# Gated scan in a two-block transformer kernel: the level products below 32 kept as strips of 32 keys, the two highest levels written without selection

## The reference

```python
def chunk_gated_scan(q, k, v, log_f, s0, with_output):
    ...
        decay = jnp.exp(jnp.where(causal, bcum[:, :, None] - bcum[:, None], -jnp.inf))
        scores = jnp.einsum('bthk,btshk,bshk->bhts', qc, decay, kc)
        o = jnp.einsum('bhts,bshv->bthv', scores, vc) + jnp.einsum(
            'bthk,bhkv->bthv', qc * jnp.exp(bcum), state)
...
    o_lf, _ = chunk_gated_scan(ql, klf, il, llf, s_cf, True)
    o_lb, _ = chunk_gated_scan(flip(ql), flip(klb), flip(il), flip(llb), s_cb, True)
```

## Time and profile before

| what | value |
|---|---|
| median of 3 runs | 2749.49 us (2744.36 to 2750.85) |
| the profiled execution, its own time | 2755.42 us |
| its span, first to last instruction | 2753.3 us |
| PE busy over the span | 2437.4 us (89%), 13690 records |
| DVE, ACT, POOL busy | 1002.5, 734.5, 198.6 us |
| mean granted PE clock | 0.910 |
| the changed block | 424.5 to 531.1 us |

### The profile page before, as it was taken

One profiled execution on the slowest core, in us unless ns is written; L12 is line 12 of the kernel. 1 busy time (PEld: TensorE's weight loads), 2 busy tenths in 40 slices (PEclk: granted clock), 3 DMA queues, 4 the chain that ended last, 5 costly groups with the idle time before them and its releaser, 6 DMA issues. The chain is left out here.

```text
span 2753.3 us, 32259 instructions
## 1 busy us (share of the span) xinstructions
PE 2437.4 (89%) x13690; PEld 1839.1 (67%) x13690; DVE 1002.5 (36%) x1585; ACT 734.5 (27%) x1271; POOL 198.6 (7%) x239
## 2 busy tenths in 40 slices
PE   6979999987999988996687999998986777799997
PEld 3533456775888866886665888886864555588885
DVE  2013118533333334635124333423225543343333
ACT  2122200023222222313212322322213552332331
POOL 0000006400000000012000000000022440000000
PEclk8988999888999997997558999998997998899999
DMA  6120013311223111200011222212210003122210
GB/s 281 38 90 17 21 41 131 145 46 47 105 79 122 69 70 62 92 31 2 4 62 62 92 92 92 92 64 92 92 33 1 1 1 123 61 92 94 110 72 31
DMA packets 16110, 196.33 MB, mean 71 GB/s; under 512 B 1888, under 2 KB 3040, under 8 KB 3936
## 3 DMA queue, kind: packets, MB, share of 16 engines
q1 hardware_dynamic: 15392, 190.72, 18.5%
q10 hardware_dynamic: 576, 3.56, 0.3%
HBM read 190.08 MB, written 2.10 MB: 70 GB/s over the span
## 5 line engine op out<-in xcount | busy, mean ns | idle before, releaser
L1503 DVE TENSOR_TENSOR wsp_mlp<-ring,wsp_mlp 128x1024 fp32r<-128x1024 f32 x128 | 156.7, 1225 | 447.8 <-ACT wsp_mlp L1474 447.8
L1474 ACT CAST wsp_mlp<-ring 128x1024 fp32r<-128x1024 f32 x128 | 133.9, 1048 | 491.4 <-PE psum L1459 489.4
L1456 PE MATMUL psum<-hs_mlp,wsp_mlp 128*128 128x512 f32 x512 | 201.7, 394 | 36.2 <-DVE wsp_mlp L1503 36.2
L1456 PE MATMUL psum<-acts_mlp,wsp_mlp 128*128 128x512 f32 x512 | 202.4, 395 | 0.0
L1458 PE MATMUL psum<-hs_mlp,wsp_mlp 128*128 128x512 f32 x512 | 201.3, 393 | 0.0
L1459 PE MATMUL psum<-hs_mlp,wsp_mlp 128*128 128x512 f32 x512 | 201.1, 393 | 0.0
L1459 PE MATMUL psum<-acts_mlp,wsp_mlp 128*128 128x512 f32 x512 | 199.3, 389 | 0.0
L1458 PE MATMUL psum<-acts_mlp,wsp_mlp 128*128 128x512 f32 x512 | 199.2, 389 | 0.0
L1503 DVE TENSOR_TENSOR wsp_ffn<-ring,wsp_ffn 128x1024 fp32r<-128x1024 f32 x66 | 80.8, 1225 | 246.2 <-ACT wsp_ffn L1474 246.2
L414 PE MATMUL psum<-hsev,wspev 128*128 128x512 f32 x672 | 156.6, 395 | 0.4 <-DVE arena_low L1647 0.3
L1456 PE MATMUL psum<-hs_ffn,wsp_ffn 128*128 128x512 f32 x352 | 138.1, 392 | 19.5 <-DVE wsp_ffn L1503 19.5
(11 more groups left out here) (391 smaller groups left out, 4152.9 us busy)
## 6 DMA issues: line engine op xcount, KB each, us to landing
ring<-weights SPq DMA_DIRECT2D x85, 2048.0 KB, 7.9
ring<-weights SPq DMA_DIRECT2D x3, 1024.0 KB, 5.7
cst<-consts ACTq DMA_DIRECT2D x1, 2209.0 KB, 14.3
xT<-xin SPq DMA_DIRECT2D x2, 1024.0 KB, 7.2
out<-xT SPq DMA_DIRECT2D x1, 2048.0 KB, 6.3
ring<-weights SPq DMA_DIRECT2D x1, 1280.0 KB, 5.9
mixT<-ctxin ACTq DMA_DIRECT2D x1, 1024.0 KB, 15.5
ring<-weights SPq DMA_DIRECT2D x2, 512.0 KB, 3.4
```

What stands on the lines that cost most here:

```text
L1456: pe.matmul(tile_bank(g, j), w_hi, src[:, 0, k0 + i, :], start=(first and i == 0), stop=False)
L1474: act.copy(wsp[:, q % 2, 0, :], raw_view(q)).then_inc(s["w_hi"], 1)
L1503: dve.tensor_tensor(wsp[:, q % 2, 1, :], raw_view(q), wsp[:, q % 2, 0, :].bitcast(F32), ALU.subtract).then_inc(s["w_lo"], 1)
```

## The change

Levels 0 to 4 keep their scores compact. A pair of halves at these levels lies within 32 tokens, so of a 128x128 chunk only the four diagonal 32x32 blocks are needed. The new tensor `w_near` (128 x 4 heads x 128) holds them: partition 32r+a is key a of strip r, column 32i+b is query b of chunk i. `near` makes them with 32 matmuls a unit, each 32 keys against 16 queries of one strip in one direction. The predicated copy goes over 128 columns with a 128x32 table `pair{lev}`. The diagonal product is made in the same layout by 16 matmuls a head instead of 4.

Levels 5 and 6 (`far`) need no selection: 16 matmuls of 32x32 and 8 of 64x64 a unit write exactly the wanted blocks into the head's bank `h`, where they stay. Ahead of level 5, `nearest` brings the compact blocks of the head to their places in the same bank, with 16 matmuls by slices of the identity. At the end ACT copies the four full banks to `wsc`. DVE no longer has a predicated copy at levels 5 and 6.

The products that update the keys are put in a helper `keys`, called by POOL with the same operands and in the same order. The arena grows by 512 columns, and the tables have 5 x 32 columns where they had 7 x 128.

```diff
+    for lev in range(5):
+        m = level_mask(lev, True) + level_mask(lev, False)
+        out[f"pair{lev}"] = np.concatenate([m[32 * r:32 * r + 32, 32 * r:32 * r + 32] for r in range(4)], axis=0)
...
+        def keys(eng, lev, h):
+            k1, _ = halves(kk[:, 0, h, :], lev)
+            _, _, (_, t2) = products_of(ff[:, 0, h, :], lev)
+            eng.tensor_tensor(k1, k1, t2, ALU.mult)
+            _, k2 = halves(kk[:, 1, h, :], lev)
+            _, _, (t1, _) = products_of(ff[:, 1, h, :], lev)
+            eng.tensor_tensor(k2, k2, t1, ALU.mult).then_inc(k_upd, 1)
...
-                        dve.wait_ge(sel_done, u - 3)
...
-                    mask = C(f"cross{lev}").bitcast(U32).rearrange("p (o n) -> p o n", o=1).to_broadcast([P, TT, P])
-                    dve.copy_predicated(wsc[:, h, :].rearrange("p (i n) -> p i n", i=TT), mask,
-                                        bank(u % 4).rearrange("p (i n) -> p i n", i=TT)).then_inc(sel_done, 1)
+                    if lev < NEAR:
+                        if lev >= 1:
+                            dve.wait_ge(sel_done, u - 3)
+                        mask = C(f"pair{lev}").bitcast(U32).rearrange("p (o n) -> p o n", o=1).to_broadcast([P, TT, 32])
+                        dve.copy_predicated(w_near[:, h, :].rearrange("p (i n) -> p i n", i=TT), mask,
+                                            bank(u % 4, P).rearrange("p (i n) -> p i n", i=TT)).then_inc(sel_done, 1)
...
-                    act.wait_ge(qf_set, h + 1)
-                    act.wait_ge(qb_set, h + 1)
-                    act.copy(wsc[:, h, :], bank(4 + h % 2)).then_inc(w_set, 1)
+                    act.copy(w_near[:, h, :], bank(4 + h % 2, P)).then_inc(w_set, 1)
                 for ch in range(4, 12):
                     mod_copy(act, ch)
+                for h in range(HH):
+                    act.wait_ge(lev_done, NU - HH + h + 1)
+                    act.copy(wsc[:, h, :], bank(h))
...
+                def near(lev, h, out):
+                    for i in range(TT):
+                        for d in (0, 1):
+                            for r in range(4):
+                                rows = slice(32 * r, 32 * r + 32)
+                                sl = slice(i * P + 32 * r, i * P + 32 * r + 32)
+                                to = halves(out[rows, 32 * i:32 * i + 32], lev)[1 - d]
+                                last = pe.matmul(to, kk[:, d, h, sl], halves(q_dec[d][:, h, sl], lev)[1 - d],
+                                                 start=True, stop=True)
+                    return last
+
+                def far(lev, h, out):
+                    half = 1 << lev
+                    for i in range(TT):
+                        for r in range(P // half):
+                            d = r % 2
+                            to = half * (r + 1 - 2 * d)
+                            last = pe.matmul(out[half * r:half * r + half, i * P + to:i * P + to + half],
+                                             kk[:, d, h, i * P + half * r:i * P + half * r + half],
+                                             q_dec[d][:, h, i * P + to:i * P + to + half], start=True, stop=True)
+                    return last
+
+                def nearest(h, out):
+                    for i in range(TT):
+                        for r in range(4):
+                            pe.matmul(out[32 * r:32 * r + 32, i * P + 32 * r:i * P + 32 * r + 32],
+                                      ident[:, 32 * r:32 * r + 32], w_near[:, h, 32 * i:32 * i + 32],
+                                      start=True, stop=True)
...
-                        pe.wait_ge(sel_done, u - 3)
-                    for i in range(TT):
-                        sl = slice(i * P, (i + 1) * P)
-                        out1, out2 = halves(bank(u % 4)[:, sl], lev)
-                        pe.matmul(out2, kk[:, 0, h, sl], halves(q_dec[0][:, h, sl], lev)[1], start=True, stop=True)
-                        last = pe.matmul(out1, kk[:, 1, h, sl], halves(q_dec[1][:, h, sl], lev)[0], start=True,
-                                         stop=True)
+                        pe.wait_ge(sel_done, min(u - 3, near_units))
+                    if lev == NEAR:
+                        nearest(h, bank(h))
+                    last = (near if lev < NEAR else far)(lev, h, bank(u % 4))
```

More of the change, by code:

```diff
@@ L100, in constants @@
     out["sooner_neg"] = np.where(a[:, None] <= a[None, :], 0.0, NEG).astype(np.float32)
-    for lev in range(LEVELS):
-        out[f"cross{lev}"] = level_mask(lev, True) + level_mask(lev, False)
+    for lev in range(5):
+        m = level_mask(lev, True) + level_mask(lev, False)
+        out[f"pair{lev}"] = np.concatenate([m[32 * r:32 * r + 32, 32 * r:32 * r + 32] for r in range(4)], axis=0)
     f32 = np.float32
@@ L238, in program @@
         epsc = sb("epsc", [P, 1])
-        ARENA = 22760
+        ARENA = 22760 + 512
         held = []
@@ L966, in program @@
         o_hg = sb("o_hg", [P, 2, T], s6)
+        w_near = sb("w_near", [P, HH, P], s6)
         k_sum = state.rearrange("p a b c -> p (a b c)")[:, 0:HH * T].rearrange("p (h n) -> p h n", h=HH)
@@ L1050, in program @@
             sem(n) for n in ("diag_done", "w_set", "qf_set", "qb_set", "lev_done", "sel_done", "q_upd", "k_upd", "t_upd"))
+        NEAR = 5
+        near_units = NEAR * HH
+        def keys(eng, lev, h):
[5 more added lines that the diff above has]
+            eng.tensor_tensor(k2, k2, t1, ALU.mult).then_inc(k_upd, 1)
         with nc.Block() as block:
@@ L1061, in _ @@
                         pool.wait_ge(k_upd, u - 3)
[L1062 to L1068, removed]
+                    keys(pool, lev, h)
             @block.vector
@@ L1093, in _ @@
                         dve.wait_ge(q_upd, u - 3)
-                        dve.wait_ge(sel_done, u - 3)
[L1095 to L1101, removed]
-                    mask = C(f"cross{lev}").bitcast(U32).rearrange("p (o n) -> p o n", o=1).to_broadcast([P, TT, P])
-                    dve.copy_predicated(wsc[:, h, :].rearrange("p (i n) -> p i n", i=TT), mask,
-                                        bank(u % 4).rearrange("p (i n) -> p i n", i=TT)).then_inc(sel_done, 1)
+                    _, q2 = halves(q_dec[0][:, h, :], lev)
+                    _, _, (t1, _) = products_of(ff[:, 0, h, 0:T], lev)
+                    dve.tensor_tensor(q2, q2, t1, ALU.mult)
+                    q1, _ = halves(q_dec[1][:, h, :], lev)
+                    _, _, (_, t2) = products_of(ff[:, 1, h, 0:T], lev)
+                    dve.tensor_tensor(q1, q1, t2, ALU.mult).then_inc(q_upd, 1)
+                    if lev < NEAR:
[4 more added lines that the diff above has]
+                                            bank(u % 4, P).rearrange("p (i n) -> p i n", i=TT)).then_inc(sel_done, 1)
                     if u >= 1:
@@ L1126, in _ @@
                     for i in range(TT):
-                        last = pe.matmul(bank(4 + h % 2)[:, i * P:(i + 1) * P], k_sum[:, h, i * P:(i + 1) * P],
-                                         hq[:, h, i * P:(i + 1) * P], start=True, stop=True)
+                        for r in range(4):
+                            sl = slice(i * P + 32 * r, i * P + 32 * r + 32)
+                            last = pe.matmul(bank(4 + h % 2)[32 * r:32 * r + 32, 32 * i:32 * i + 32], k_sum[:, h, sl],
+                                             hq[:, h, sl], start=True, stop=True)
                     last.then_inc(diag_done, 1)
```

## The result

The changed kernel takes 2732.3 us in the median (2726.4 to 2735.7, 6 runs) against 2745.8 for the kernel before on the same chip (2744.0 to 2750.9, 6 runs): ratio 0.9942, 95% interval 0.9928 to 0.9957. It is faster: 13.5 us by the medians, 12 to 20 us by the interval; 12.1 were forecast. The profiled execution is 2732.3 us (span 2730.3).

What follows compares the result with a forecast made beforehand. PE was taken as the bound, with DVE and POOL taking turns just under it. Savings of 3.4 + 9.7 + 0.4 - 2 + 0.6 = 12.1 us took the median from 2749.5 to 2737.5 us, range 2728 to 2750.

Steps and rivals of the forecast that it cites:

- The likeliest case: In the level loop the bound goes from PE to DVE and POOL taking turns: 12.1 us gained, chance 0.62.
- the signs that the prediction named for being wrong: POOL and DVE still waiting over 20 us for PE, pauses cutting the records, or granted clock under 0.9 in the stage.
- Levels 0 and 1: 8 x 0.43 = 3.4: In eight units where DVE was full, each select shortened by 0.43 us shortens the stage: 3.4 us off.
- the third rival: DVE gains little because its products meet POOL's and wait, 3 x 1.1 us: gain 6, 2743 us, chance 0.08.
- Levels 2 to 6: 9.7, less 2 for pauses: Twenty units at DVE's and POOL's turns take 58.6 us against 68.3; PE's pauses at chunk changes give 2 back.
- PE's price: Levels 0 to 4: 64 product records a unit at 0.015 us, 0.96 us against 1.79; 0.45 if record count cost nothing.
- the rival of instruction supply (0.13): PE stays the bound by its instruction count, 0.029 us a record with pauses every 128: gain 6.8, 2743 us, chance 0.13.
- The clock (0.17): Granted clock halves inside the stage: for part of it 2743 to 2750 us (0.10), for most of it slower (0.07).
- ACT's four last copies: Four 512-element copies at the stage's end, 0.58 us each, hidden beside DVE's and POOL's last units; uncovered, worth 0.8 us.
- The tables: 368 KB less to load in the opening stage: 0.6 us off, at most 0.88, at least nothing.
- The last turn: At the end of the level loop the last turn is no longer waited for: 0.4 us off.
- POOL's share: POOL's busy share of the level loop rises from 67% to over 75%.

Runs made afterwards that it cites:

- e2: The changed kernel with both products that update the keys moved from POOL to DVE: 2724.0 us, ratio 0.9930.
- e4: The kernel before with its predicated copy cut from 512 to 128 columns, leaving out three of four chunks' scores: 2744.5 us, ratio 1.0001.
- e5: The changed kernel with strips of 64 keys instead of 32 at levels 0 to 4, select over 256 columns: 2738.4 us, ratio 0.9967.
- e6: The changed kernel with strips of 64 keys at levels 0 to 4 and both key products on DVE: 2718.4 us, ratio 0.9886.
- e8: The changed kernel with the tables padded by 736 unused columns to their old size: 2727.3 us, ratio 0.9930.
- e3: The changed kernel with the products of levels 0 to 4 issued twice into the same place: 2759.0 us, ratio 1.0055.
- e1: The kernel before with only the products of levels 5 and 6 changed, levels 0 to 4 as before: 2737.1 us, ratio 0.9968.
- e7: The changed kernel with key products on DVE and products of levels 0 to 4 for two of four chunks only: 2716.8 us, ratio 0.9880.
- e11: e6 with 32 tiny matmuls, result unused, added after each unit of levels 0 to 4: 2765.7 us, ratio 1.0066.

## Why the prediction was right, and where it was not

*The verdict and the size.* 12.1 us were forecast and 12 to 20 found, 2737.5 against 2732.3. The stage was to take 95 us and takes 89.4. The likeliest case was the right one, that the bound goes from PE to DVE and POOL. But the nearness of the sum is luck. Levels 0 and 1 gave 2.9 us less than forecast, levels 2 to 6 some 8.7 more, and outside the stage some 4 us were lost again, for which the sum has no term. Two of the signs that the prediction named for being wrong did show: pauses cut the records, and the clock's column says 0.88 in levels 0 and 1. The waits for PE, 12.4 us of POOL and 7.7 of DVE, are together just at the 20 us it named as a third.

*Levels 0 and 1: 8 x 0.43 = 3.4. This step failed.* The selects take 0.29, as worked out. But the step held that DVE, being full, wins what its select loses. DVE was full because its three products with both inputs in SBUF mostly wait for the POOL product under way; a shorter select makes the shrink begin sooner and wait longer. The changed kernel's shrink at 437.82 is 0.46 longer than the one in the earlier trace rows, and the mean of seven in levels 0 and 1 went from 1.13 to 1.65 us. PE was no longer the pace there (DVE and POOL waited 0.8 and 0.9 us for it), and the part still took 38.1 us instead of 38.7; with the turns gone, in e2, it took 29.5. e4 shows the same longer shrinks from the select alone. It is what the third rival said of a single unit; I gave it 0.08 and 3 x 1.1 us of wait.

*Levels 2 to 6: 9.7, less 2 for pauses. The turns were mis-sized.* 58.6 us were forecast for 20 units, 2.93 each. Undisturbed units take 2.52 in levels 2 and 3 (467.28 to 469.79), 2.25 in level 4 and 2.1 in level 6 by the starts of DVE's first products, so by an estimate from these 8 x 2.52 + 4 x 2.25 + 8 x 2.1 = 46. My 1.15 and 1.09 for POOL's two products already held their waits for DVE's two, and I then added DVE's 0.28 for each once more. POOL's product that waits for nobody takes 0.85, and it is DVE's beside it that waits:

```profile
492.94 0.85 POOL L1062 TENSOR_TENSOR arena<-arena 128x384 f32<-128x384 f32 x1
492.96 1.11 DVE L1103 TENSOR_TENSOR hT<-hT,arena 128x256 f32<-128x256 f32 x1
```

The 51.3 measured are some 5 more than these 46. I put them down to PE's pauses and the lowered clock, by difference and not by a run; for pauses I had set 2, and with another cause, the chunk changes.

*PE's price.* A near record is 0.0088 us and not 0.015, a unit's 64 thus 0.56 and not 0.96. "It can't be much less than half that" was about right. But the term's condition, that no run of 128 comes about since modulation steps stand between, was wrong: the pauses come 127 records apart, or a multiple of that, with modulation steps counted in. So the rival of instruction supply (0.13) is true as a mechanism, at a smaller size, because PE has 2.5 us a unit and needs 0.56 + 1.76. In e2, where DVE is fast, PE with its pauses and 17.1 us at half clock is the bound.

*The clock (0.17).* It fell in three places, together 13.7 of 89.4 us, where 1.00 was forecast. What that cost here no run shows. In e5, where 34 us ran at half clock with PE busy throughout, the stage was 7 us longer than with strips of 32. In e6, with the same strips and 0.9 us at half clock, it was 19 us shorter than in e5, but there the keys had moved to DVE too.

*What lies beside.* ACT's four last copies (0.61 each) run from 508.8 to 510.9, DVE's last work ends at 510.5, the next stage's first matmul starts at 511.16: the copies are hidden, as said, but for 0.4 us at most. The keys helper moved nothing. The tables were put at 0.6, which e8 neither confirms nor refutes. The last turn and POOL's share (82%, 72.6 of 88.7) came as forecast; POOL's wait of 12.4 us was to be under 10, PE waits 3.2 us for DVE and POOL instead of 10, presumably since its lead is spent in pauses.

*Starts, pauses and turns.* The starts at 0.0088 us are a third of the 25 ns that the Trainium skill (TensorE: Matmul & The Clock Gate, the section on 56 against 53.3 ns) gives as the least; this trace does not bear that out for strips. On the pauses, the Trainium skill (Runtime: NRT & Kernel Launch, Instruction fetch mechanics) says that instructions come in blocks of 256 and that crossing into the next is mostly hidden. The block fits, since 128 f32 records with their loads are 256 instructions, the pauses come 127 records or a multiple apart, and e3's 2560 added instructions brought ten more packets. "Mostly hidden" doesn't: seven pauses of 1.3 to 4.1 us on PE's matmuls come to 16.6 us in this stage. The turns of DVE and POOL agree with the Trainium skill (SBUF — State Buffer, Who interferes with whom), which speaks of an exclusive lock: POOL's product begun at 438.71 took 1.88 us beside DVE's shrink, against 0.85 where it waits for nobody.

## What to carry to other kernels

Where DVE and POOL take turns, shortening what one of them does outside the turns gave nothing in levels 0 and 1. What helped was to put the products together on the faster of the two (0.5 us for 384 columns on DVE, 0.85 on POOL), and then to cut PE. Small matmuls save array time, but many short records bring pauses of some 2 us that give part of it back: strips of 64 keys beat strips of 32 by 11 us of stage once DVE had the keys. And PE's clock may fall for tens of microseconds (34 in e5), so a cut on a busy PE is measured, not added up.

## What the runs showed of the hardware

- Where f32 records have few columns, PE pauses for 1.3 to 4.9 us with no semaphore behind it. In the stage of all kernels there are 50 such pauses of over 1.2 us (under "issue"), and from each to the next in its kernel PE does 126 to 128 matmul records or, within two, a whole multiple of 127. The kernel before, e1, e4, e5 and e6 have none, e7 has three, e2 six, the changed kernel seven. In the stage there are 15 packets on the instruction queue against 6 before; in the whole program 118 against 109:

```profile
q8 instruction: 118, 1.93, 0.3%
```

  e3 has 128, ten more for 2560 more instructions, each of 16,384 bytes. Of the 50 pauses, 48 end 2.2 to 2.8 us after such a packet begins. So the pause looks like a wait for instructions; the packets' timing alone was not varied.
- Records of 128x32 weights and 16 moving columns start 0.0088 us apart at full clock.
- The clock fell to 0.50 after 3.5 us with 13 records (e5) and stayed there for 34 us though PE was busy for 33 of them; in e11 it was there for 81.9 us of the stage, in two stretches. In the changed kernel three falls lasted 3.4 to 6.8 us. Why it stays so long isn't settled.
- With DVE alone at them, query products are 0.42 us and key products 0.56; in turns, in the changed kernel, 0.41 to 1.41 on DVE and 0.84 to 2.31 on POOL.
